# Rotary half-turns by DMA instead of matmuls, and output-norm chains in two halves of the tokens

## The reference, cut to what matters

```python
def rms_norm_2(x, gain):
    xf = x.astype(jnp.float32)
    y = xf * lax.rsqrt(jnp.mean(xf * xf, axis=-1, keepdims=True) + RMS_EPS)
    return y.astype(x.dtype) * gain

def rope(x, positions):
...
    x1, x2 = xf[..., :half], xf[..., half:]
    return jnp.concatenate([x1 * cos - x2 * sin, x2 * cos + x1 * sin], axis=-1).astype(x.dtype)

def compress_blocks(k, pe, w1, b1, w2):
...
    return jax.nn.gelu(flat @ w1 + b1, approximate=True) @ w2
```

## Time and profile before

| what | value |
| --- | --- |
| median of 3 runs | 3034.61 us (3032.1 to 3035.51) |
| profiled execution, its own time | 3034.25 us |
| its span, first to last instruction | 3032.5 us |
| PE (matmul) busy | 2998.2 us, 99% of the span |
| DVE busy | 1774.3 us, 59% |
| ACT busy | 1269.7 us, 42% |
| POOL busy | 146.0 us, 5% |
| mean granted TensorE clock | 0.992 of full |

### The profile page before, as it was taken

The page is one execution under the profiler, slowest core; times in us unless marked ns, Lnnn a source line. Parts: engine busy times, 40 slices in busy tenths (PEclk is TensorE's granted clock), DMA queues, the critical chain, the costliest instruction groups (busy, mean ns, idle before and its releaser), DMA issues.

```text
span 3032.5 us, 37840 instructions
## 1 busy us (share of the span) xinstructions
PE 2998.2 (99%) x14648; PEld 2400.0 (79%) x14648; DVE 1774.3 (59%) x3128; ACT 1269.7 (42%) x2377; POOL 146.0 (5%) x203
## 2 busy tenths in 40 slices
PE   9999999999999999999999999999999999999998
PEld 7778888877888888888876678888787766788886
DVE  4666775345555577634465557775364655577743
ACT  4444443322333344432366545443233655355431
POOL 0000000000000000001001101000020011010000
PEclk9999999999999999999999999999999999999999
DMA  4222322222222333333211132222232111223332
GB/s 156 71 94 94 99 97 97 98 77 84 84 77 88 93 98 97 98 97 98 92 36 43 48 99 80 101 97 98 84 102 88 36 42 49 90 84 105 98 97 70
DMA packets 72035, 260.35 MB, mean 86 GB/s; under 512 B 8112, under 2 KB 8112, under 8 KB 71728
## 3 DMA queue, kind: packets, MB, share of 16 engines
q1 hardware_dynamic: 70992, 254.52, 26.3%
q10 hardware_dynamic: 864, 3.41, 0.3%
HBM read 255.81 MB, written 2.10 MB: 85 GB/s over the span
## 4 chain that ended last, share of the span: by engine, by line
PE 93%; DVE 4%; ACT 2%; issue 1%; DMA 0%; POOL 0%; DVEq 0%; SPq 0%; ACTq 0%
PE bank L473 25%; PE bank L476 24%; PE bank L480 24%; PE bank L550 2%; PE bank L554 2%; PE bank L551 2%; PE bank L630 2%; PE bank L662 2%; PE bank L644 1%; PE bank L793 1%; PE bank L910 1%; DVE wl L1377 1%; DVE big L1961 1%; PE bank L940 1%; ACT big L1356 1%
## 5 line engine op out<-in xcount | busy, mean ns | idle before, releaser
L1377 DVE TENSOR_TENSOR wl<-ring,wh 128x512 fp32r<-128x512 f32 (+1 forms) x946 | 648.9, 692 | 829.2 <-ACT wh L996 824.4
L473 PE MATMUL bank<-xh,wh 128*128 128x512 f32 x2464 | 989.0, 401 | 14.1 <-ACT wh L996 7.2
L476 PE MATMUL bank<-xh,wl 128*128 128x512 f32 x2464 | 966.4, 392 | 0.3 <-DVE wl L1377 0.3
L480 PE MATMUL bank<-xl,wh 128*128 128x512 f32 x2464 | 926.2, 391 | 0.0
L996 ACT ACTIVATE wh<-ring 128x512 fp32r<-128x512 f32 (+1 forms) x946 | 581.0, 622 | 814.3 <-PE bank L480 734.7
L473 PEld LDWEIGHTS bank<-xh,wh 128*128 128x128 f32 x2464 | 466.3, 189 | 148.9 <-issue 38.4
L480 PEld LDWEIGHTS bank<-xl,wh 128*128 128x128 f32 x2464 | 465.1, 189 | 99.9 <-DVE xl L1470 0.4
L476 PEld LDWEIGHTS bank<-xh,wl 128*128 128x128 f32 x2464 | 466.9, 189 | 91.7 <-DVE wl L1377 1.3
L473 PE MATMUL bank<-bigr,wh 128*128 128x512 f32 x1024 | 399.0, 390 | 0.6 <-ACT bigr L1360 0.6
L476 PE MATMUL bank<-bigr,wl 128*128 128x512 f32 x1024 | 398.5, 389 | 0.0
L480 PE MATMUL bank<-bigr,wh 128*128 128x512 f32 x1024 | 393.4, 389 | 0.0
(11 more groups left out here) (203 smaller groups left out, 2756.5 us busy)
## 6 DMA issues: line engine op xcount, KB each, us to landing
ring<-in_w_up SPq DMA_DIRECT2D x176, 512.0 KB, 3.5
ring<-in_w_down SPq DMA_DIRECT2D x88, 512.0 KB, 3.4
ring<-in_w_in SPq DMA_DIRECT2D x64, 512.0 KB, 3.5
ring<-in_w_ret SPq DMA_DIRECT2D x32, 512.0 KB, 3.3
ring<-in_w_even SPq DMA_DIRECT2D x19, 512.0 KB, 3.3
ring<-in_w_ret_v SPq DMA_DIRECT2D x16, 512.0 KB, 3.3
ring<-in_w_ret_out SPq DMA_DIRECT2D x16, 512.0 KB, 3.3
ring<-in_w_proj SPq DMA_DIRECT2D x16, 512.0 KB, 3.5
```

The source lines that it names most:

```text
L473: e.matmul(o, K.wh(p, c * 128, 128), oh, start=start, stop=False, skip_group_check=True)
L476: e.matmul(o, K.wl(p, c * 128, 128), oh, start=False, stop=False, skip_group_check=True)
L480: m = e.matmul(o, K.wh(p, c * 128, 128), ol, start=False, stop=stop, skip_group_check=True)
L1377: e.tensor_tensor(K.wl(i, 0, w), K.raw(i), K.wh(i, 0, w).bitcast(F32), ALU.subtract).then_inc(F.lo.tell(("piece", i)), 1)
```

## The change

**Rope.** The matrix "rot" and its 14 matmuls go. SP issues, for each turned tile, four transfers of 32 partitions x 512 from tmp to a tile `turned(r)` in PP, which swap the halves (`half_turn`); the sign goes into the constant `invf` from which the sine is made. The transfers stand in SP's queue between weight units: turns 0 and 1 ahead of the unit behind the first w1 unit, 2, 3 and 4 ahead of the next ones, 5 and 6 three units later. DVE's sine product and POOL's cosine product wait for the transfers. DVE's ropes 5 and 6 stand later than before.

**Output norms.** Sums, power and spread are made in two halves of the tokens, in banks 2 and 3. For tile 0 of the next projection DVE's m and x and ACT's xh are made in halves of 256, and PE's first ten matmuls become twenty of 256 columns. ACT copies the spread row into an SBUF tile RSB by halves, and for tiles 1 to 7 DVE's m reads RSB in place of the bank. The last seam is cut in the same way.

```diff
+    def half_turn(l, r):
+
+        q.wait_ge(F.dve, ("ra", l, r))
+        for a, b in ((0, 32), (32, 0), (64, 96), (96, 64)):
+            e.dma_start(K.turned(r)[a:a + 32, :], K.tmp(2 * r % 4)[b:b + 32, :]).then_inc(
+                K.turning(r).tell(*([("rot", l, r)] if a == 96 else []), by=16), 16)
+
+    turns = {}
+    for l in range(2):
+        u = W.raws["w1", l, 0]
+        turns.update({u + 1: (l, (0, 1)), u + 2: (l, (2,)), u + 3: (l, (3,)), u + 4: (l, (4,)), u + 7: (l, (5, 6))})
     for u, (src, width, pieces) in enumerate(W.units):
+        if u in turns:
+            for r in turns[u][1]:
+                half_turn(turns[u][0], r)
...
-    def group(key, nk, operand, banks, hooks):
+    def group(key, nk, operand, banks, hooks, border=False):
...
+            if border and k == 0:
+                s = ("f", key[1]) if key[0] == "up" else key[:2]
+                for a in range(2):
+                    q.wait_ge(F.act, ("xh", s, 0, a))
+                    for m, b in enumerate(banks):
...
+                        high(half(BK[b], a), *parts[m], half(K.xh(0), a), a == 0)
+                ol = operand[1](k)
+                for m, b in enumerate(banks):
+                    low(BK[b][:, :], *parts[m], ol, False)
+                continue
...
-        sums(s, 6 % 3, apart=7 % 3)
-        spread(s, 64, 3, F.dve, ("added", s))
...
+        for i in range(NQ):
+            if i % 2 == 0:
+                q.wait_ge(F.pool, ("rsn", s, i // 2))
+            m = e.matmul(BK[2 + i // 2][:, i * 128:(i + 1) * 128], bc(K.SM[:, 64 + i:65 + i], [[0, 128]]), K.cs("ident"),
+                         start=True, stop=True, skip_group_check=True)
+            if i % 2:
+                m.then_inc(F.stat.tell(("spread", s, i // 2)), 1)
+        vacated[2] = vacated[3] = [(F.act, ("rs", s))]
...
-            e.matmul(BK[b][:, :], K.cs("rot"), K.tmp(2 * r % 4), start=True, stop=True).then_inc(F.attn.tell(("rot", l, r)), 1)
-            vacated[b] = [(F.dve, ("rb", l, r))]
...
-        rotated(0)
-        rotated(1)
         tile(("n", l, 6), DT, xn(s), F.dve)
-        rotated(2)
-        rotated(3)
         tile(("n", l, 7), DT, xn(s), F.dve)
-        rotated(4)
...
-            if i == 0:
-                rotated(5)
-                rotated(6)
...
+    def half_row(s, a):
+
+        q.wait_ge(F.stat, ("spread", s, a))
+        q.wait_ge(F.dve, ("m", s, 0, a))
+        e.activation(half(K.RSB, a), half(BK[2 + a], a), ACT.Copy, bias=0.0, scale=1.0).then_inc(
+            F.act.tell(("rsh", s, a), *([("rs", s)] if a else [])), 1)
...
+            if j == 0:
+                for a in range(2):
+                    half_row(before, a)
+                    q.wait_ge(F.dve, ("x", s, 0, a))
+                    e.activation(half(K.xh(0), a), half(K.x(0), a), ACT.Copy, bias=0.0,
...
-            e.scalar_tensor_tensor(out=M[j], in0=M[j], scalar=K.vec(gain, gi + j), in1=BK[3][:, :], op0=ALU.mult,
-                                   op1=ALU.mult).then_inc(F.dve.tell(("m", s, j), *([("added", s)] if j == DT - 1 else [])), 1)
-            q.wait_ge(F.dve, ("m", s, j))
-            e.tensor_tensor(K.x(j), K.x(j), M[j], ALU.add).then_inc(F.dve.tell(("x", nxt, j)), 1)
+                for a in range(2):
+                    half_scale(s, key, M, K.vec(gain, gi), a)
+                    q.wait_ge(F.dve, ("m", s, 0, a))
+                    e.tensor_tensor(half(K.x(0), a), half(K.x(0), a), half(M[0], a), ALU.add).then_inc(
+                        F.dve.tell(("x", nxt, 0, a)), 1)
+            else:
+                q.wait_ge(F.act, ("rs", s))
+                e.scalar_tensor_tensor(out=M[j], in0=M[j], scalar=K.vec(gain, gi + j), in1=K.RSB[:, :], op0=ALU.mult,
+                                       op1=ALU.mult).then_inc(F.dve.tell(("m", s, j)), 1)
...
         def rope(r):
-            q.wait_ge(F.attn, ("rot", l, r))
-            e.tensor_tensor(K.tmp(2 * r % 4 + 1), BK[2 + (r + 1) % 2][:, :], K.ROPE[:, S:2 * S], ALU.mult).then_inc(
-                F.dve.tell(("rb", l, r)), 1)
+            q.wait_ge(K.turning(r), ("rot", l, r))
+            e.tensor_tensor(K.turned(r), K.turned(r), K.ROPE[:, S:2 * S], ALU.mult).then_inc(F.dve.tell(("rb", l, r)), 1)
...
             if i == 0:
-                rope(5)
                 lo_to(W.first["tm", l] + 2)
-                rope(6)
...
         lo_to(p + 3)
+        rope(5)
+        rope(6)
...
-        e.scalar_tensor_tensor(out=XM[j], in0=XM[j], scalar=K.vec("g_post_ffn_2", 8 + j), in1=BK[3][:, :], op0=ALU.mult,
-                               op1=ALU.mult).then_inc(F.dve.tell(("m", s, j)), 1)
+        if j == 0:
+            for a in range(2):
+                half_scale(s, ("down", 3), XM, K.vec("g_post_ffn_2", 8), a)
+        else:
+            q.wait_ge(F.act, ("rs", s))
+            e.scalar_tensor_tensor(out=XM[j], in0=XM[j], scalar=K.vec("g_post_ffn_2", 8 + j), in1=K.RSB[:, :], op0=ALU.mult,
+                                   op1=ALU.mult).then_inc(F.dve.tell(("m", s, j)), 1)
```

More of the change, by code:

```diff
@@ L45, with half @@
 FLAGS = ("proj", "stat", "attn", "hi", "act", "lo", "dve", "pool", "land0", "land1", "land2", "land3",
-         "x0", "first", "x1", "x2", "x3", "x4", "gain", "cst", "vec", "pos", "dil", "ret", "out")
+         "rot0", "rot1", "x0", "first", "x1", "x2", "x3", "x4", "gain", "cst", "vec", "pos", "dil", "ret", "out")
+def half(ap, a):
+    return ap[:, a * S // 2:(a + 1) * S // 2]
 class Flag:
@@ L611, in fills @@
         return fill
-    half = [None]
+    held = [None]
     def soft(L, steps, fill, upto):
@@ L649, in soft @@
                 step = steps[t - 3]
-                q.wait_ge(F.act, half[0])
+                q.wait_ge(F.act, held[0])
                 if step.cmp is not None:
@@ L666, in soft @@
                 if step.done is not None:
-                    half[0] = step.done
+                    held[0] = step.done
     def cmp_turn(l, j):
@@ L744, in ffn @@
         turn[0] = [0, 1, 4, 5, 6, 7]
-        group(("up", f, "g"), DT, xn(s), [next_bank() for _ in range(5)], {} if late else norm(s))
+        group(("up", f, "g"), DT, xn(s), [next_bank() for _ in range(5)], {} if late else norm(s), late)
         for i in range(5, 2 * FT):
@@ L943, in sb_pv @@
             if kt == 0 and kv == 1:
-                half[0] = ("os", l, j)
+                held[0] = ("os", l, j)
         for t in range(16 + 2):
@@ L958, in tensor_program @@
         fill(10 ** 6)
-        vacated[4] = [(F.act, half[0])]
+        vacated[4] = [(F.act, held[0])]
         def merged(k):
@@ L1269, in scalar_program @@
         s = ("n", l)
-        group(("n", l, "g"), 5, post_feed(s) if l else nothing, {} if l else {3: lambda: rs_row(s)})
+        group(("n", l, "g"), 5, post_feed(s, ("p", 0, "f")) if l else nothing,
+              {} if l else {3: lambda: rs_row(s)})
         if l:
@@ L1692, in rotate @@
                 q.wait_ge(F.act, ("oh", 4 * h - 5))
-        for i, (half, c) in enumerate(((0, K.cosr), (1, K.sinr), (0, K.sinr), (1, K.cosr))):
+        for i, (part, c) in enumerate(((0, K.cosr), (1, K.sinr), (0, K.sinr), (1, K.cosr))):
             events = [("rt", h, which, i)]
@@ L1696, in rotate @@
                 events += [("freed", *key) for key in keys]
-            e.tensor_tensor(K.tmp(i), K.bank(keys[half])[:, :], c, ALU.mult).then_inc(F.dve.tell(*events), 1)
+            e.tensor_tensor(K.tmp(i), K.bank(keys[part])[:, :], c, ALU.mult).then_inc(F.dve.tell(*events), 1)
     def centre(h):
@@ L1991, in root, with half_roots @@
             F.pool.tell(("rsn", s)), 1)
+    def half_roots(s):
+        for a in range(2):
+            q.wait_ge(F.dve, ("ms", s, a))
+            e.tensor_tensor(K.SM[:, 64 + 2 * a:66 + 2 * a], K.SM[:, 2 * a:2 * a + 2], K.cs("mhalf", 2), ALU.pow).then_inc(
+                F.pool.tell(("rsn", s, a)), 1)
     s = ("e",)
```

86 lines of the change are left out of this document (54 added, 32 removed).

## The result

Sixteen runs of each: 3038.36 us median after the change (3030.77 to 3043.15) against 3033.88 before (3029.07 to 3035.51), a ratio of 1.0014 with a 95% interval of 1.0008 to 1.0021. So the kernel is slower by some 4.5 us, clear of the noise of this comparison, though within the 0.2% that the prediction called the same. 3019.2 was forecast, and 3010 to 3027 was the range. The executions also spread wider than before, over 12.4 us in place of 6.4.

A forecast was written before the change was run, and what follows sets the result against it. PE was taken as the bound, busy 99% of the 3032.5 us span. Terms of -12.0 + 1.9 - 8.0 + 3.0 = -15.1 us gave a forecast of 3019.2 us, range 3010 to 3027.

The forecast's parts named there:

- term 2: Rotations by transfers: PE waits before the second hybrid layer's first compression half, none in the first layer; +1.9 us.
- term 4: Three inner seams, DVE's side: m from RSB waits for POOL, xl of tile 6 limits PE's gain; -8.0 us.
- Term 1: Fourteen rotation matmuls leave PE, where nothing hides them; -12.0 us.
- Rival C: Compression: unparted 32-column matmuls bring the clock down, some 2.5 us a layer lost, 3024 us; chance 0.13.
- Term 3: Inner seams, PE's side: shorter idle stretch and clock partly back; PE alone gains 2.0 to some 3.9 us in the first.
- rival B: Seams: m isn't held by POOL, they give up to 12.5 us; 3011, or 3013 with part of the hold; chance 0.22.
- Term 5: Last seam: m of tiles 1 to 7 reads RSB and is held by POOL's adds; +3.0 us.
- D: Turns land late, first compression half and PE's tiles 6 and 7 wait: slower than before; chance 0.05.
- E: Only one half works: rotations gained, seams nothing since the DVE side eats all; 3027 us; chance 0.10.

The follow-up runs named there:

- e5: Changed kernel plus four 512-column matmuls with unused result on PE ahead of the second hybrid layer's first compression half; 3032.24 us, ratio 0.9998.
- e6: Kernel before the change, with rotations 5 and 6 moved behind both compression halves; 3041.03 us, ratio 1.0024.
- e7: Changed kernel with the spread row in a bank for tiles 1 to 7, compression halves in banks 2 and 3, SP's turns moved; 3028.37 us, ratio 0.9983.
- e1: Kernel before the change with the rope part of the diff alone, output norms as they were; 3034.88 us, ratio 1.0002.
- e3: Changed kernel with the two compression halves written to the free banks 2 and 3; 3031.76 us, ratio 0.9997.
- e4: Changed kernel with the spread row left in a bank for tiles 1 to 7, without ACT's copies; 3026.85 us, ratio 0.9980.
- e10: e7 with the turn of tile 4 behind one more weight unit and DVE's rope 4 and scaling of tile 6 behind wl pieces; 3018.55 us, ratio 0.9950.

## Why the prediction was wrong, step by step

Two terms failed, and each missed by 10.7 us: term 2, where a stand-still of PE was priced at its own length and the clock behind it at nothing, and term 4, where the slack was read from the wrong item.

**Term 1, rotations, -12.0: right.** In the first layer PE's starts differ by 4.35 us (5.95 less the 1.6 of chance) where five rotations are gone, and by 2.03 more where the other two are. In the second layer other waits lie over it.

**Term 2, the transfers, +1.9: the chain right, its size short, and its sequel missed.** The chain was the one described, down to the scaling of tile 4. Counted from the first scaling (2229.24 now, 2230.87 before), PE reached the bank after 11.5 us, as taken, but the scaling of tile 4 ended after 14.9 and not 13.6, since a turn took 3.85 us and not 3.3: an issue costs SP 0.60 and not 0.33. So PE waited 3.45 and not 1.9, within the bounds given (0 to 7). But the prediction priced this stand-still at its own length. Behind it the clock is at 1.2 GHz for all but the first 2 us of the compression and 3 us more. That costs 5.8 by the table; e5, which fills the idle time and leaves the rest, got 4.6 back in its profile and some 6 in the medians. With 3.3 us in the first layer, where the prediction had no wait and no loss, the term is +12.6 where 1.9 stood.

**Rival C had the place, half of the price (2.5 us a layer) and the wrong cause.** It said that the unparted small matmuls bring the clock down. e5, e6 and e7 show 7.66 us of them at full clock. What the profile of before did show, and the prediction used only in the seams, is that the clock falls where PE has stood still. The small matmuls come in after that: behind the seams, where 256- and 512-column matmuls ran, full clock was back 3.0 to 5.7 us after the restart, while here it wasn't within 12.4 us of 32-column ones. Why it stays down there is not shown. For the first layer it stays open which of two waits behind the compression (0.88 and 0.34 us in the changed kernel; 0.99 and 0.49 in e1) set off the fall: e3 and e5 had 0.38 and 0.29 there and no fall, yet e4 had 0.83 there, and e5 0.87 in the second layer, and no fall either.

**Term 3, PE's side of the seams: right.** In the first seam the restart came 1.95 us sooner (4.77 for 6.72), where 2.2 were taken, and half clock lasted 3.0 us behind it in place of 4.7. In the second the restart came 1.64 sooner and half clock lasted 4.5 for 5.6; in the third 2.87 sooner, with the spread at 1.48 us for 2.07, and half clock was as long as before, 5.7 for 5.6. All of it lies between nothing and all of the clock coming back, as said.

**Term 4, DVE's side, -8.0: the hold right, the slack wrong, and with it the sign of the result.** Two-SBUF-input products and POOL's adds do exclude each other, with 0.43 per tile and not 0.7. The rows of m in the inner seams read 0.74, as rival B had it, and yet B is wrong: POOL's add waited for m, and the x sum behind m for POOL, so that the tile pays all the same. But the prediction let PE wait on xl of tile 6 and reckoned with its slack of 5.1 us. The tighter item was the first wl piece behind the last xl, with a slack of 0.84 in the first seam, which none of the prediction's rows shows. DVE came 1.58 later to it than before, less than the 2.7 taken for xl, and this alone turns the gain of 2.3 into a loss of some 0.8. And again the clock came on top: the stops of 0.84 and 2.20 us in the first seam cost 3.0 plus 1.7 for the clock behind the second. The three seams made +2.7. e4 bears the cause out: with m from a bank, the period is 3.20, and 11.5 us come back, the last seam's included. What the Trainium skill states of the shared SBUF interface ("GPSIMD Engine Reference", section "Specifications") agrees with the trace: 1.67 and 1.24 us for the sum with POOL beside it, 0.69 alone. What the prediction made of it in time, 8.0 gained in place of 12.5, erred for the reasons above.

**Term 5, the last seam, +3.0: right in kind, +1.95 measured** from the sums to the end, with 2.93 for 1.92 in each of three periods, so 3.0 in all, where 3.9 were taken. The first m starts 2.1 us sooner behind its sums than before and the second, which has to wait for the row in SBUF, 1.1 sooner.

**The sum.** By the two profiles: -12.4 for rotations, +3.3 and +9.3 for the compression of the two layers, +2.7 seams, +2.0 last seam, -1.6 that were chance near 36 us, in all +3.3, where the spans differ by +2.8. That e10 measures 3018.55, next to the 3019 of the forecast, is chance: it reads the row from a bank and has other gains and losses than the forecast was added up from. The rivals missed too: D and E each held one wait at its own length, and no rival had a wait and the clock behind it in one. The advice of the Trainium skill against two transfers to disjoint partition halves ("DMA: Bandwidth & Descriptors", section "Rules for kernel authors") fits the 0.60 us that each of the four issues costs; whether fewer transfers for a turn would be faster, no run here shows.

## What to carry to other kernels

Price a new stand-still of TensorE at its length and add what the clock may lose behind it, by what runs there. In this kernel full clock was back 3.0 to 5.7 us after a seam's restart, with wide matmuls, and not within 12.4 us of 32-column ones. Where a stop of 3.45 us couldn't be avoided, matmuls that nothing reads were worth some 6 us. When a chain in front of an engine is made shorter, look for the slack of every stream that feeds that engine afterwards, and take the smallest (0.84 us here, and not 5.1). Keep one operand of VectorE in PSUM where GpSimd works beside it: that was worth 11.5 us. Transfers queued between weight loads delay these: in e3 and e7 another unit came too late, by 1.09 us and by up to 3.84.

## What the hardware showed that I had not expected

- An issue of a 32 x 512 fp32 transfer between SBUF tiles took SP 0.59 us in the median (0.51 to 1.69), one of a 512 KB weight unit 0.33, or 0.47 right behind such transfers. From issue to landing the 64 KB took 2.0 us in the median (1.9 to 3.8), the same as the output's 256 KB.
- POOL and DVE exclude each other both ways: POOL's 1.29 became 1.72 when DVE's product with two SBUF inputs had started first, and its cosine product went from 1.27 to 1.70.
- The granted clock was still 1.00 during a stand-still of 3.45 us and fell only 2 us into the matmuls behind it (1.4 us in e1). In e4 it fell 0.2 us ahead of them.
- The clock fell behind stops of 2.49 us in both layers of e6 and behind one of 2.20 us in the changed kernel, and not behind its stops of 2.35 and 2.09 us.
